# A diffusion backbone step on one core: a fourth modulation half tile asked for at once, the conditioning turned first, the filter network moved into the projections

## What is computed

```
def adaln(cond, w, b):
    ada = jax.nn.silu(cond) @ w + b                  # 1024 -> 6 * 1024, per layer
    return [ada.reshape(..., 6, D_MODEL)[:, :, None, :][:, i] for i in range(6)]
sh1, sc1, g1, sh2, sc2, g2 = adaln(cond, w_ada[l], b_ada[l])
h = rmsnorm(x, norm_mix[l]) * (1.0 + sc1) + sh1
q = (h @ w_q) ; k, v = split(h @ w_kv) ; q, k = rmsnorm per head, then axial rotation (latent)
...
hdn = sin(freq * (feats @ w1 + b1)) ; hdn = sin(freq * (hdn @ w2 + b2))   # implicit filters, layer 1
```

## Time and profile before

| | us |
|---|---|
| median of 3 runs | 1278.89 (1277.01 to 1280.53) |
| the profiled execution, its own time | 1278.2 |
| its span, first to last instruction | 1276.4 |
| TensorE busy | 1094.6 (86%) |
| VectorE busy | 470.9 (37%) |
| ScalarE busy | 257.2 (20%) |
| first projection starts | 45.49 |
| mean granted TensorE clock | 0.932 of full |

### The profile page before, as it was taken

One profiled execution on the slowest core, in us unless ns is written; L12 is line 12 of the kernel. 1 busy time (PEld: TensorE's weight loads), 2 busy tenths in 40 slices (PEclk: granted clock), 3 DMA queues, 4 the chain that ended last, 5 costly groups with the idle time before them and its releaser, 6 DMA issues.

```text
span 1276.4 us, 14669 instructions
## 1 busy us (share of the span) xinstructions
PE 1094.6 (86%) x5453; PEld 577.4 (45%) x5453; DVE 470.9 (37%) x1002; ACT 257.2 (20%) x498; POOL 185.9 (15%) x209
## 2 busy tenths in 40 slices
PE   5799888987998889999789999989866988778865
PEld 3344555555443334443345565658752422222213
DVE  3356566134233112333363337792440111111116
ACT  3211344022333023323231110000221100000001
POOL 1020000002241113231100002130021222222100
PEclk9899999987999899999889999999877989989987
DMA  9996986432999559999960200505420899999933
GB/s 353 404 325 261 259 322 227 190 132 70 369 395 403 204 212 382 399 402 411 330 236 1 99 1 0 231 0 198 163 92 14 340 414 413 413 412 406 411 144 133
DMA packets 94241, 324.54 MB, mean 254 GB/s; under 512 B 17647, under 2 KB 33423, under 8 KB 77380
## 3 DMA queue, kind: packets, MB, share of 16 engines
q1 hardware_dynamic: 71936, 303.49, 61.4%
q0 software_dynamic: 15504, 13.37, 3.3%
q10 hardware_dynamic: 6708, 6.45, 1.4%
HBM read 333.22 MB, written 30.11 MB: 285 GB/s over the span
## 4 chain that ended last, share of the span: by engine, by line
PE 64%; DMA 19%; DVE 7%; issue 3%; ACT 3%; SPq 3%; POOL 0%; ACTq 0%; POOLq 0%; DVEq 0%
PE bank L844 15%; DMA ring<-in_moe_w_up 10%; PE bank L992 10%; PE bank L858 6%; PE bank L660 3%; PE bank L1031 3%; PE bank L776 3%; DMA ring<-in_w_ada 3%; DMA hT<-in_hy_log_decay 3%; PE bank L563 3%; PE bank L598 2%; PE bank L1020 2%; PE bank L978 2%; DMA ring<-in_moe_w_down 2%; PE bank L791 2%
## 5 line engine op out<-in xcount | busy, mean ns | idle before, releaser
L844 PE MATMUL bank<-ring,work 128*64 128x512 f32 x1120 | 268.9, 636 | 42.4 <-issue 36.3
L844 PEld LDWEIGHTS bank<-ring,work 128*64 128x64 f32 x1120 | 82.7, 146 | 220.0 <-issue 215.8
L858 PE MATMUL bank<-ring,work 128*64 128x512 f32 x560 | 129.2, 604 | 4.2 <-DVE work L1627 1.6
L992 PE MATMUL bank<-hT,ring 128*128 128x384 f32 x384 | 128.0, 494 | 5.3 <-ACT hT L1128 5.3
L1639 DVE SCALAR_TENSOR_TENSOR work<-bank,work 128x256 f32<-128x256 f32 x32 | 15.5, 484 | 261.0 <-ACT work L1224 261.0
L992 PEld LDWEIGHTS bank<-hT,ring 128*128 128x128 f32 x384 | 74.0, 194 | 58.0 <-issue 9.8
L858 PEld LDWEIGHTS bank<-ring,work 128*64 128x64 f32 x560 | 37.5, 138 | 74.0 <-issue 63.3
L1224 ACT ACTIVATE work<-bank 128x256 f32<-128x256 f32 x32 | 12.3, 384 | 247.5 <-PE bank L844 247.5
L1651 DVE COPY work<-bank 128x512 f32<-128x512 f32 x32 | 22.1, 692 | 106.5 <-PE bank L858 106.5
L1788 POOL DMA_INDIRECT work<-token_vectors,work x28 | 28.7, 1026 | 187.2 <-PE bank L827 172.5
L563 PE MATMUL bank<-ring,condS 128*32 128x256 f32 x768 | 47.0, 397 | 8.8 <-DVE ada L1328 5.5
(11 more groups left out here) (263 smaller groups left out, 1505.2 us busy)
## 6 DMA issues: line engine op xcount, KB each, us to landing
ring<-in_moe_w_gate SPq DMA_DIRECT2D x32, 2048.0 KB
ring<-in_moe_w_up SPq DMA_DIRECT2D x32, 2048.0 KB
ring<-in_moe_w_down SPq DMA_DIRECT2D x32, 2048.0 KB
ring<-in_w_ada SPq DMA_DIRECT2D x24, 2048.0 KB, 13.4
ring<-in_hy_w_in SPq DMA_DIRECT2D x6, 2048.0 KB, 19.8
filter_spectra<-work ACTq DMA_DIRECT2D x8, 768.0 KB
work<-expert_rows SPq DMA_DIRECT2D x16, 384.0 KB, 6.6
ring<-filter_spectra SPq DMA_DIRECT2D x2, 3072.0 KB, 12.0
```

The source lines that it names most:

```text
L844: last = mm(bank[2][WIN * j:WIN * (j + 1), :], gt[:, k, WIN * j:WIN * (j + 1)], gu[:, :, j, k, :], start=(k == 0), stop=(k == KD - 1))
L858: last = mm(bank[b + hf][WIN * j:WIN * (j + 1), :], AT[:, k, WIN * j:WIN * (j + 1)], dn[:, j, k, hf * HALF:(hf + 1) * HALF], start=(k == 0 ...
L992: last = mm(bank[n % 2][:, 0:T], w[:, k, (n % 4) * P:(n % 4 + 1) * P], hT[:, k, :], start=(k == 0), stop=(k == KD - 1))
```

## The change

- Half tile 3 goes to slot 2, the later home of the second half of the query weights, and is asked for at once with half tiles 0 to 2. From half tile 4 on slots 3 to 5 are used in turn as before.
- The query weights come in two transfers. The second is asked for when half tile 3 has been multiplied. The order of the Sync queue is now: half tiles 0 to 3, key/value weights, first half of the query weights, half tile 4, second half of the query weights, half tile 5, the three small transfers, half tile 6.
- The conditioning columns are turned, copied and passed to ScalarE ahead of the tokens.
- Tile 1 has its own bank (7), so `ada_mm(1)` waits for no `ada_done`.
- The filter network moves into the steps of the projections: `mlp(0)` at `m == 0`, `mlp(1)` at `m == 5`, in bank 3.
- Tiles 2 to 6 are multiplied one step later: at `m` = 2, 4, 6, 8, 10.
- The stores of keys and values are counted by `y_out`.

```diff
         def ada_rows(h):
-            return ring_slot(3 + h % 3).rearrange("p (k n) -> p k n", k=KD // 2)
+            return ring_slot(2 if h == 3 else 3 + ada_place(h)).rearrange("p (k n) -> p k n", k=KD // 2)
+        def ada_place(h):
+            return h if h < 4 else (h - 1) % 3
+        def ada_came(h):
+            return sem(f"ada_in{ada_place(h)}"), 16 * (1 if h < 4 else (h - 1) // 3 + 1)
...
-        ADA_QK = {1: 2, 3: 3, 5: 4, 7: 5, 9: 6}
+        ADA_QK = {2: 2, 4: 3, 6: 4, 8: 5, 10: 6}
+        MLP_QK = {0: 0, 5: 1}
...
-        XT_BANK = [0, 1, 2, 6]
+        XT_BANK = [0, 1, 4, 6]
...
         def load_ada(sp, h):
-            if h >= 3:
-                sp.wait_ge(sem("ada_half"), h - 2)
+            if h >= 4:
+                sp.wait_ge(sem("ada_half"), h - 3 if h < 7 else h - 2)
...
-            for h in range(3):
+            for h in range(4):
                 load_ada(sp, h)
             sp.dma_start(wkv, a["attn_w_kv"][0].rearrange("(k p) n -> p k n", p=P)).then_inc(sem("wkv_in"), 16)
-            load_ada(sp, 3)
-            sp.dma_start(wq, a["attn_w_q"][0].rearrange("(k p) n -> p k n", p=P)).then_inc(sem("wq_in"), 16)
+            wq_v = a["attn_w_q"][0].rearrange("(k p) n -> p k n", p=P)
+            sp.dma_start(wq[:, 0:KD // 2], wq_v[:, 0:KD // 2]).then_inc(sem("wq_in"), 16)
+            load_ada(sp, 4)
+            sp.wait_ge(sem("ada_half"), 4)
+            sp.dma_start(wq[:, KD // 2:], wq_v[:, KD // 2:]).then_inc(sem("wq_in"), 16)
+            load_ada(sp, 5)
...
-            for h in range(4, 7):
-                load_ada(sp, h)
+            load_ada(sp, 6)
...
             def ada_mm(t):
 
-                if t >= 1:
+                if t >= 2:
                     pe.wait_ge(sem("ada_done"), t)
...
-            pe.wait_ge(sem("filt_small_in"), 16 * 6)
-            mm(bank[4][0:FH, 0:T], w1, C["feats"][0:FEAT, :], start=True, stop=True).then_inc(sem("mlp_mm"), 1)
             pe.wait_ge(sem("cond_set"), 2)
             ada_mm(0)
             ada_tr(0)
-            pe.wait_ge(sem("mlp_done"), 1)
-            pe.wait_ge(sem("pc_done"), 2)
-            mm(bank[5][0:FH, 0:T], w2[:, :], hd1[0:FH, 0, :], start=True, stop=True).then_inc(sem("mlp_mm"), 1)
             ada_mm(1)
             ada_tr(1)
...
             for m in range(QK + 2):
                 if m < QK:
                     qk_mm(m)
+                if m in MLP_QK:
+                    mlp(MLP_QK[m])
...
             qk_root(act, fn, QK - 1)
+            adaR_copy(ADA_QK[QK])
...
-            angle(0)
             normalise(0)
             ada_add(0)
-            angle(1)
             ada_add(1)
             scale_shift(0, 0, 0)
...
                 if m - 1 in ADA_QK:
                     ada_add(ADA_QK[m - 1])
+                if m in MLP_QK:
+                    angle(MLP_QK[m])
```

More of the change, by code:

```diff
@@ L473, in _ @@
             sp.dma_start(a["out_3"][0, 0].rearrange("h s d -> s h d"), V[:, 0, :].rearrange("p (h d) -> p h d", h=NKV))\
-                .then_inc(sem("kv_out"), 16)
+                .then_inc(sem("y_out"), 16)
             sp.wait_ge(sem("ktok_done"), 1)
             sp.dma_start(a["out_2"][0, 0].rearrange("h s d -> s h d"), ktok.rearrange("p (h d) -> p h d", h=NKV))\
-                .then_inc(sem("kv_out"), 16)
+                .then_inc(sem("y_out"), 16)
             for h in range(17, 2 * NADA):
@@ L523, in _ @@
                 sp.dma_start(y_out[c], yout[:, c, :]).then_inc(sem("y_out"), 16)
-            sp.wait_ge(sem("y_out"), 16 * TC)
-            sp.wait_ge(sem("kv_out"), 32)
+            sp.wait_ge(sem("y_out"), 16 * TC + 32)
         @block.tensor
@@ L533, in _ @@
             pe.wait_ge(sem("ident_in"), 16)
+            n = R_END - 2 * P
+            pe.wait_ge(sem("early_in"), 16 * (len(early_rows) + 4))
+            tr(bank[7][:, 0:n], prow[0:n, 2, :], ident[0:n, 0:n]).then_inc(sem("pc_mm"), 1)
             pe.wait_ge(sem("x_in"), 16 * TC)
@@ L550, in ada_bank @@
             def ada_bank(t):
-                return bank[2] if t < ADA_CORE[0] else bank[7]
+                return bank[2] if t < ADA_CORE[0] and t != 1 else bank[7]
             def ada_mm(t):
-                if t >= 1:
+                if t >= 2:
                     pe.wait_ge(sem("ada_done"), t)
@@ L636, in _, with mlp @@
             ada_tr(0)
-            pe.wait_ge(sem("mlp_done"), 1)
-            pe.wait_ge(sem("pc_done"), 2)
-            mm(bank[5][0:FH, 0:T], w2[:, :], hd1[0:FH, 0, :], start=True, stop=True).then_inc(sem("mlp_mm"), 1)
             ada_mm(1)
             ada_tr(1)
+            def mlp(i):
+                if i == 0:
+                    pe.wait_ge(sem("filt_small_in"), 16 * 6)
+                    pe.wait_ge(sem("rt_done"), 1)
+                    mm(bank[3][0:FH, 0:T], w1, C["feats"][0:FEAT, :], start=True, stop=True).then_inc(sem("mlp_mm"), 1)
+                else:
+                    pe.wait_ge(sem("mlp_done"), 1)
+                    mm(bank[3][0:FH, 0:T], w2[:, :], hd1[0:FH, 0, :], start=True, stop=True).then_inc(sem("mlp_mm"), 1)
             pe.wait_ge(sem("wkv_in"), 16)
@@ L1079, in adaR_copy @@
                     act.wait_ge(sem("ada_tr"), t - 1)
-                b = bank[2] if t < ADA_CORE[0] else bank[7]
+                b = bank[2] if t < ADA_CORE[0] and t != 1 else bank[7]
                 fn(ada_row(t), b[:, 0:256], ACT.Copy).then_inc(sem("adaR_set"), 1)
@@ L1166, in probT_copy @@
                 if j == 2:
-                    act.wait_ge(sem("kv_out"), 32)
+                    act.wait_ge(sem("y_out"), 32)
                     act.wait_ge(sem("tab_clear"), 16 * DEPTH)
@@ L1290, in _ @@
             link(v.memset(minus[0:1, :], 0.0))
+            dve.wait_ge(sem("pc_mm"), 1)
+            v.tensor_copy(pc[:, 2 * P:R_END], bank[7][:, 0:R_END - 2 * P]).then_inc(sem("pc_done"), 1)
             for k in range(KD):
@@ L1469, in probT_copy @@
                 if j == 2:
-                    dve.wait_ge(sem("kv_out"), 32)
+                    dve.wait_ge(sem("y_out"), 32)
                     dve.wait_ge(sem("tab_clear"), 16 * DEPTH)
```

18 lines of the change are left out of this document (7 added, 11 removed).

## The result

| | before | after |
|---|---|---|
| median of the runs, us | 1279.13 (5 runs) | 1291.54 (5 runs, 1288.89 to 1294.38) |
| span of the profiled execution, us | 1276.4 | 1289.8 |
| ratio of the times | 1 | 1.0093, 95% interval 1.0072 to 1.0114 |
| first projection starts | 45.49 | 37.52 |
| the projection of step 3 starts | 69.81 | 72.93 |

The three starts are us from the beginning of the profiled execution. The changed kernel is slower by 12.4 us. Its first projection starts 8 us sooner. At the projection of step 3 the lead has become a lag of 3.1 us, and by the output projection the lag is 13.45 us.

The account below looks back on a forecast made before the run. TensorE was taken to be on most of the chain that ended last. Terms 1.4 + 2.2 + 0.8 + 4.8 + 2.2 + 1.3 = 12.7 us on 1278.2 gave 1290.9, plus 0.7 for the median: 1291.5 us, range 1284 to 1295.5.

Parts of the forecast that it names:

- first projection starts: Key/value projection at the start: begins at about 37.3 instead of 45.49, some 8 us sooner.
- small transfers there: Before VectorE's first raw copy: cached keys, cos and sin all landed (`cache_in` complete) at about 60.3 us.
- step 3 against the earlier trace, clock left out: Projection of step 3: starts at 71.2 where it started at 69.81, +1.4 us, because step 2 waits for `cache_in`.
- slow restart of step 2: Projection of step 2: runs at lowered clock after TensorE's idle time, +2.2 us within bounds 0 and 2.65.
- `mlp(1)`: Filter network matmul at `m == 5`, new between projections: +0.8 us.
- wait for `ada_add(5)`: End of the projections: the product of tile 6, with no projection ahead of it, waits for VectorE's addition, +4.8 us.
- slow product of tile 6: End of the projections: its 64 matmuls run at clock 0.50 after the idle time, +2.2 us within bounds 0 and 2.65.
- product moved past two matmuls: Tile 6's product, now behind `qk_ss(8)` and `qk_rot(7)`, delays later half tiles that attention waits for, +1.3 us.
- rival D: Attention: the longer wait for tile 17 brings a third clock fall, up to 2.65 us more; at 2, 1293.5; chance 0.12.
- Rival A: Step 2: small transfers overtake, so it starts at 52.7; about 1281 us, without slow restart not slower; chance 0.10.
- Rival B: Step 2 and tile 6's product: the clock stays up at both restarts, 8.3 us slower, 1287; chance 0.12.
- Rival C: Expert stage: the delay is partly taken back where it waits for transfers, 0 to 9 us; chance 0.06.

Follow-up runs that it names:

- a1: Changed kernel, but VectorE waits for the three small transfers only at the first turn in step 2, not ahead of its first raw copy; 1281.07 us.
- a2: Changed kernel, but in step 9 VectorE adds the bias of tile 5 right behind its raw copy, ahead of norm and turn; 1284.83 us.
- a4: Changed kernel with six unneeded matmuls put into TensorE's wait ahead of the product of tile 6; 1288.26 us.
- a3: Changed kernel with the edits of a1 and a2 together; 1274.57 us, 0.9964 of the kernel before.
- a8: The same kernel as a3, run again on another occasion; 1273.26 us, 0.9971 of the kernel before.
- a5: Changed kernel with the old table of products (tiles 2 to 6 at steps 1, 3, 5, 7, 9); 1283.37 us.
- b1: Kernel before with one edit, the three small transfers asked for behind half tile 5; 1276.23 us, 0.9984 of the kernel before.
- a6: a3 with the second half of the output weights asked for behind half tile 17 instead of ahead of it; 1274.53 us.
- a9: The same kernel as a6, run again beside a8; 1272.6 us, 0.9961 of the kernel before.
- a7: a6 with half tile 18 also asked for ahead of the second half of the output weights; 1270.5 us, 0.9952 of the kernel before.

## Why the prediction was right

1291.5 us were forecast, 1291.54 measured; that the two agree to 0.1 us is luck, since the executions lie between 1288.89 and 1294.38. What counts is the terms ("clock left out" is the lag of 3.1 us without the 2.8 of the slow projection):

| term | forecast | in the profile | shown by |
|---|---|---|---|
| first projection starts | 37.3 | 37.52 | trace |
| small transfers there | 60.3 | 59.1 | trace |
| step 3 against the earlier trace rows, clock left out | +1.4 | +0.3 | trace |
| slow restart of step 2 | +2.2 | +2.8 | trace |
| both together, against no wait | 10.2 less without (a1's expectation) | 10.5 less in the median, 10.8 at step 3 | a1 |
| `mlp(1)` | +0.8 | +0.79 | trace |
| wait for `ada_add(5)` | +4.8 | +4.69 | a2 |
| slow product of tile 6 | +2.2 | +2.29 | a4 |
| product moved past two matmuls | +1.3 | +1.2, see below | trace |
| slow product behind the wait for half tile 17 | rival D | +1.2 | trace, this pair of profiles |

**The small transfers.** They came 1.2 us sooner than forecast. The count of bytes took the moment when TensorE went on behind half tile 5. In the kernel before about 22.7 MB had been moved by then (376 GB/s over 60.3 us), probably a part of half tile 6 among them, which was asked for right behind; here 22.4 MB were enough (379 GB/s over 59.1 us). By these estimates 0.7 of the 1.2 us are bytes that `cache_in` didn't need and 0.5 is rate. The slow restart was 0.6 us dearer than taken, and 0.14 above the upper bound of 2.65. The errors cancelled in part: step 3 at +3.1 instead of +3.6. Rival A, that they overtake the weights, is out: the DMA view shows the second half of the query weights at 52.1, half tile 5 at 57.4, cached keys at 57.2 and cos and sin at 59.1. The cached keys, issued behind half tile 5, landed within 0.2 us of it.

**The last product.** The earlier trace rows gave the wait to 0.1 us, because the rows of step 8 hold the same chain of engines as step 9 and only what TensorE does meanwhile differs.

**The 1.3 us and attention.** The forecast said that half tile 17 hangs on the end of the product of tile 6. Nine profiles bear it out. From the end of that product to the end of the wait for half tile 17: 39.5 us before, 39.1 after, 39.2 in a1, 39.7 in a2, 39.6 in a3, 39.8 in a8, 38.9 in a4, 39.5 in a5, 39.5 in b1 (end of the product, start plus duration, against the start of the second half of the product of tile 8); and a6, which takes half the output weights out from between, ends that wait. The end of the product came 12.40 us later than before, the end of the wait 12.08; the four terms ahead of it (3.12, 0.79, 4.69, 2.29) make 10.9, and the other 1.2 are this term. But the forecast for the size of the wait was wrong: 3.5 to 4 us were expected, 2.47 seen. TensorE took 1.1 us longer to get there (19.00 us between the starts of the products of tiles 7 and 8, 17.93 before), and with these the wait would have been 3.5. As a3 and a8 show, this time varies between executions of one kernel, and the wait with it (3.77 and 2.75 us). The clock of the changed kernel was down twice in that stretch, around 172 (0.50) and from 164 to 168 (0.58, the row below); that of the kernel before once, around 159 (0.51).

```profile
164.00:168.00 4.00, 3.63 (x19) 2.51 (x15) 2.64 (x8) 1.00 (x3) 0.00 (x0) 0.58 1.02 201
```

**Rival B** (the clock stays up) fell at both places, by the 8.17 and 5.95 us of the trace and by a4. The Trainium skill (TensorE: Matmul & The Clock Gate, Part 1) says of modelling that the ramp is under 1% of a typical span and not to be fitted to a count of slow matmuls. The two slow groups together are 5.1 us, 0.4% of this span, which agrees with its size; but without them the sum would have been 8.3 us, 1287, and 12.4 were measured.

**Rival D** (a third fall of the clock) came, but not by the condition it was given. Behind the wait for half tile 17 the second half of the product took 3.15 us where it takes 1.93; the wait, though, hadn't grown (2.47 and 2.55). Nor does its length decide: in a4 it was 3.22 us and the half product took 1.93 us, in b1 it was 2.17 us and took 3.52, and b1 is the kernel before but for the place of the small transfers. So these 1.2 us belong to this pair of profiles and not surely to the change. Measured, the terms of the sum of 12.7 come to 12.1; with the 1.2 they give 13.3 of the 13.4 us by which the spans differ. The medians differ by 12.4, and the executions scatter by more than the 1 us between the two.

**Rival C** (taken back by the experts' transfers) is excluded for this pair of profiles by the constant 13.4 us, and beyond it by the medians of a1 and a2: they fell by 10.5 and 6.7 us, where TensorE reached the output projection 10.8 and 6.4 us sooner.

**A step that was only half right** is the one on the filter network: "the next product of step 6 covers them" held in the changed kernel, but a5, where step 6 has no product, paid 3.18 us and was misjudged by that.

## What to carry to other kernels

When a start is made earlier, list every wait between it and the work behind it, and see which of them used to be free. A count that several transfers share and that an in-order engine waits for ahead of its first use makes the whole stage wait for the last of them; wait where the datum is first read. And when a table shifts work by one step, look at its last entry: what covered each wait may not exist there. The two waits of TensorE, 8.4 and 4.7 us, cost 2.8 and 2.3 us on top of themselves, and a4 took these 2.3 us back by filling the wait; a wait of 2.2 to 3.8 us in attention cost between 0 and 1.7 us more, with no order by its length.

## What the runs showed of the hardware

The output weights, four transfers onto 64 partitions each, pass at half the rate. In the kernel before, by stretches:

```profile
131.00:140.00 9.00, 8.62 (x39) 7.16 (x40) 7.60 (x9) 1.34 (x5) 0.00 (x0) 1.00 1.02 415
...
148.00:156.00 8.00, 5.21 (x65) 3.17 (x57) 5.54 (x19) 3.90 (x14) 0.00 (x0) 1.00 1.03 208
```

The last two figures are the DMA engines' busy share and the GB/s: full both times, 415 GB/s with modulation weights on 128 partitions, 208 with the output weights. Other layouts weren't tried, so that the 64 partitions are the cause is argued and not shown.

An issue on the Sync engine can take long: that of the first half of the query weights, behind four half tiles and the key/value weights, took 16.34 us in the changed kernel, that of the second half 0.37 us. It did no harm, since the DMA engines were busy throughout (407 GB/s from 10 to 28). That a full queue holds the issue is the likely reason and was not tested.

Not settled is why a profile's experts' stage of layer 0 (from the router to the start of the Hyena layer) took 376.3 us in the kernel before and in the changed one, 375.9 in a3 and 378.6 to 379.3 in a1, a2, a5 and a6, while a8, a3's twin, took 377.9 and a9, a6's twin, 376.3 (a4 378.4, a7 378.3, b1 375.9). Since a3 and a8 are one kernel and differ by 2 us, and a6 and a9 by 3, a difference of this size lies between executions; what sets it stays open.
